# W_q of head 2 read into two places ahead of the gathers, its queries behind head 1's, and head 0's scores copied ahead of half 1's exponentials

## What is computed

```python
def chunk(xc):                      # 128 positions, x2 after its RMS norm
    q = (xc @ w_query).reshape(128, 8, 2, 128)
    sc = jnp.einsum('chpd,hpnd->chpn', q, sub_keys)
    s1, i1 = lax.top_k(sc[:, :, 0], 16)
    s2, i2 = lax.top_k(sc[:, :, 1], 16)
    # the 16 best of the 256 sums s1 + s2 name 16 of 16384 experts
    best, pos = lax.top_k(cand, 16)
    experts = jnp.take_along_axis(cand_idx, pos, axis=-1)
    g = jax.nn.softmax(best, axis=-1)
    h = gelu(einsum('cd,chkd->chk', xc, u[experts]))
    return einsum('chk,chkd->cd', h * g, v[experts])
```

## Time and profile before

| | us |
|---|---|
| median of 3 runs | 840.93 |
| lowest and highest run | 838.71, 841.11 |
| the profiled execution's own time | 836.34 |
| its span, first to last instruction | 834.5 |
| PE busy, of the span | 679.0 (81%) |
| DVE busy | 525.5 (63%) |
| POOL busy | 502.4 (60%) |
| ACT busy | 236.6 (28%) |
| bytes moved by DMA | 297.91 MB, 268.47 of them by the gathers |

### The profile page before, as it was taken

The page is one execution under the profiler, slowest core; times in us unless marked ns, Lnnn a source line. Parts: engine busy times, 40 slices in busy tenths (PEclk is TensorE's granted clock), DMA queues, the critical chain, the costliest instruction groups (busy, mean ns, idle before and its releaser), DMA issues.

```text
span 834.5 us, 7478 instructions
## 1 busy us (share of the span) xinstructions
PE 679.0 (81%) x2205; PEld 369.6 (44%) x2205; DVE 525.5 (63%) x1389; ACT 236.6 (28%) x606; POOL 502.4 (60%) x533
## 2 busy tenths in 40 slices
PE   5999997469978988878888989887776667777776
PEld 4877575435435444335444445443332223333332
DVE  5565169279652867576667676657666757665454
ACT  7567244232311432311212222331212121212110
POOL 5000007447773777777777767777777776777751
PEclk9999998599997999999999999999999999999999
DMA  8955108949999999999999999999999999999994
GB/s 326 310 166 185 53 1 305 376 143 404 409 403 390 400 409 409 407 409 410 408 409 409 409 409 409 411 409 409 409 410 408 410 409 409 409 409 409 409 409 180
DMA packets 92121, 297.91 MB, mean 357 GB/s; under 512 B 8737, under 2 KB 17074, under 8 KB 92082
## 3 DMA queue, kind: packets, MB, share of 16 engines
q0 software_dynamic: 73728, 268.47, 81.5%
q1 hardware_dynamic: 18354, 28.98, 10.1%
HBM read 296.36 MB, written 1.05 MB: 356 GB/s over the span
## 4 chain that ended last, share of the span: by engine, by line
DMA 34%; PE 34%; POOL 15%; issue 7%; DVE 6%; ACT 4%; DVEq 0%; SPq 0%; POOLq 0%; ACTq 0%
DMA v_row<-in_peer_v_dram,expert 23%; PE bank L1372 16%; POOL u_row L446 9%; DMA u_row<-in_peer_u_dram,expert 7%; POOL v_row L457 6%; PE xg L1119 5%; PE bank L1290 4%; DMA wq<-in_peer_w_query_dram 3%; PE bank L1244 3%; DVE u_row L1023 2%; PE bank L1185 1%; PE bank L1168 1%; ACT soft L549 1%; DMA x_sb<-in_x_dram 1%; ACT L700 0%
## 5 line engine op out<-in xcount | busy, mean ns | idle before, releaser
L1372 PE MATMUL bank<-v_row,diag 128*128 128x512 f32 x1000 | 475.7, 622 | 110.8 <-DMA v_row<-in_peer_v_dram,expert 94.7
L1023 DVE CUSTOM_DVE_ANT_0 u_row<-u_row,xg 128x1024 f32<-128x1024 f32 x244 | 296.4, 1220 | 186.2 <-DMA u_row<-in_peer_u_dram,expert 178.5
L1372 PEld LDWEIGHTS bank<-v_row,diag 128*128 128x128 f32 x1000 | 189.3, 198 | 353.9 <-issue 320.1
L446 POOL DMA_INDIRECT u_row<-in_peer_u_dram,expert x256 | 246.4, 962 | 148.0 <-DVE expert L999 70.5
L457 POOL DMA_INDIRECT v_row<-in_peer_v_dram,expert x256 | 241.2, 942 | 113.3 <-issue 56.6
L1290 PE MATMUL bank<-featT,wq 128*128 128x128 f32 x512 | 68.8, 294 | 23.1 <-DMA wq<-in_peer_w_query_dram 22.2
L1290 PEld LDWEIGHTS bank<-featT,wq 128*128 128x128 f32 x512 | 68.3, 210 | 38.0 <-DMA wq<-in_peer_w_query_dram 23.2
L700 ACT ACTIVATE h_gelu<-h_dot 128x4 f32<-128x4 f32 x64 | 12.8, 202 | 251.8 <-DVE h_dot L1023 251.7
L707 ACT ACTIVATE diag<-ident,act_w 128x128 f32<-128x128 f32 x250 | 82.5, 389 | 3.6 <-DVE act_w L1036 3.6
L660 ACT ACTIVATE qT<-bank 128x128 f32<-128x128 f32 x32 | 8.9, 277 | 176.7 <-PE bank L1290 176.7
L356 POOL TENSOR_TENSOR normed<-qk_raw,t_qk_rs 128x512 f32<-128x512 f32 x4 | 4.1, 1047 | 56.6 <-DVE t_qk_rs L896 56.6
(11 more groups left out here) (160 smaller groups left out, 518.0 us busy)
## 6 DMA issues: line engine op xcount, KB each, us to landing
w_raw<-in_w_in_dram SPq DMA_DIRECT2D x12, 1024.0 KB, 7.9
wq<-in_peer_w_query_dram SPq DMA_DIRECT2D x8, 1024.0 KB, 18.1
w_raw<-in_w_out_dram SPq DMA_DIRECT2D x4, 1024.0 KB, 5.1
u_row<-in_peer_u_dram,expert POOLq DMA_INDIRECT x256, 16.5
v_row<-in_peer_v_dram,expert POOLq DMA_INDIRECT x256, 16.6
x_sb<-in_x_dram SPq DMA_DIRECT2D x2, 512.0 KB, 3.8
g_row<-in_norm_g_dram SPq DMA_DIRECT2D x1, 512.0 KB, 12.9
out_dram<-y_rows SPq DMA_DIRECT2D x1, 512.0 KB, 6.7
```

The lines of the kernel that those rows point to most:

```text
L446: pool.indirect_dma_start(u_rows[n % U_RING][:, :], None, peer_u[0], bass.IndirectOffsetOnAxis(ap=expert[:, u, s:s + 1], axis=0))\
L1023: dve.tensor_tensor_reduce(out=row[:, :], in0=row[:, :], in1=x_of, scale=1.0, scalar=0.0, op0=ALU.mult, op1=ALU.add, accum_out=h_dot[:, u ...
L1372: ins = mm(ps[y_bank(h, c)][:, :], diag[:, m % DIAG_RING, :], v_rows[n % V_RING][:, c * COLS:(c + 1) * COLS], start=False, stop=True, skip ...
```

## The change

SP reads W_q of head 2 a second time: into `wq_2`, two parts of 4 KB per partition at the places of x (half 0) and of qt (half 0), as soon as the last transposes of half 0's attention output are done (`mixT_done` 2). PE does `head_queries(2)` directly behind `head_queries(1)` from these parts, and ACT copies its queries and scores directly behind those of head 1. The place of `wq[2]` for half 1 moves to the output projection's weights; those of heads 3 and 4 take the two places that are free after `values_done`. The v row buffers are taken in another order, with other waits on POOL. On ACT `scores_evac(0)` and `scores_evac(1)` go ahead of `exponentials(4)`.

```diff
--- before.py
+++ after.py
@@ -65,6 +65,7 @@
 UNIT_GROUPS = TOPK // GROUP
 SBUF_X_GROUPS = 3
 PROBS = 9
+BATCHES = 12
 PROBS_BANK = [2, 2, 3, 5, 5, 0, 1, 0, 1]
 MIXES_READY = {0: 1, 3: 2, 4: 3}
 MIX_AFTER = {0: 0, 4: 1, 6: 4}
@@ -190,13 +191,14 @@
     diag = Region(sq_at).put("diag", [P, DIAG_RING, P])
 
 
-    wq_at = [wh_at, wl_at, v_at, e_at] + [wr_at + 8 * K * i for i in range(4)]
+    wq_at = [wh_at, wl_at, wr_at, v_at, e_at] + [wr_at + 8 * K * i for i in range(1, 4)]
     wq = [Region(at).put(f"wq{i}", [P, KD, 2 * P]) for i, at in enumerate(wq_at)]
+    wq_2 = [Region(at).put(f"wq2_{c}", [P, KD, P]) for c, at in enumerate((x_at, qt_at))]
 
 
     u_at = [w + 8 * K + 4 * K * i for w in (wh_at, wl_at) for i in range(4)] + [xn_at + 8 * K, xn_at + 12 * K]
     u_rows = [Region(at).put(f"u_row{i}", [P, D]) for i, at in enumerate(u_at)]
-    v_row_at = [skn_at, skn_at + 4 * K, x_at, qt_at, qt_at + 4 * K, kt_at, kt_at + 4 * K, probs_at, scaled_at]
+    v_row_at = [skn_at, skn_at + 4 * K, kt_at, kt_at + 4 * K, qt_at + 4 * K, probs_at, x_at, qt_at, scaled_at]
     v_rows = [Region(at).put(f"v_row{i}", [P, D]) for i, at in enumerate(v_row_at)]
     y_rows = [Region(x_at + 4 * K).put("y_rows0", [P, D]), Region(u_at[0]).put("y_rows1", [P, D])]
     added = Region(u_at[1]).put("added", [P, D])
@@ -217,6 +219,7 @@
         sk_loaded = sem("sk_loaded")
         w_loaded = [sem(f"w_loaded{i}") for i in range(W_LOADS)]
         wq_loaded = [sem(f"wq_loaded{i}") for i in range(PEER_HEADS)]
+        wq_2_loaded = sem("wq_2_loaded")
         g2_loaded = sem("g2_loaded")
         u_landed = [sem(f"u_landed{i}") for i in range(U_RING)]
         v_landed = [sem(f"v_landed{i}") for i in range(V_RING)]
@@ -396,11 +399,15 @@
             sp.wait_ge(w_used, 10)
             query_weights(0)
             query_weights(1)
+            sp.wait_ge(mixT_done, 2)
+            for c in range(2):
+                sp.dma_start(wq_2[c][:, :, :], w_query[0, :, 512 + c * P:512 + (c + 1) * P].rearrange("(k p) n -> p k n", p=P))\
+                  .then_inc(wq_2_loaded, 16)
             sp.wait_ge(values_done, PROBS)
-            query_weights(2)
             query_weights(3)
+            query_weights(4)
             sp.wait_ge(x2_done, 4)
-            for i in range(4, PEER_HEADS):
+            for i in (5, 6, 7, 2):
                 query_weights(i)
 
 
@@ -470,8 +477,12 @@
                     for n in range(g * GROUP - LAG, (g + 1) * GROUP - LAG):
                         if n == 0:
                             pool.wait_ge(skT_done, 4)
-                        if n == 4:
+                        if n == 2:
+                            pool.wait_ge(logits_done, BATCHES)
+                        if n == 5:
                             pool.wait_ge(values_done, PROBS)
+                        if n == 6:
+                            pool.wait_ge(query_done, 6)
                         if n == 8:
                             pool.wait_ge(xg_in_psum, 2)
                             pool.wait_ge(u_used, SBUF_X_GROUPS * GROUP)
@@ -667,9 +678,9 @@
             skT_evac(1)
             query_evac(0)
             query_evac(1)
-            exponentials(4)
             scores_evac(0)
             scores_evac(1)
+            exponentials(4)
             exponentials(5)
             act.wait_ge(late_v_done, 1)
             act.activation(v_sb[:, 0, 1, :], ps[5][:, :], ACT.Copy).then_inc(copied, 1)
@@ -677,6 +688,10 @@
             query_evac(3)
             scores_evac(2)
             scores_evac(3)
+            query_evac(4)
+            query_evac(5)
+            scores_evac(4)
+            scores_evac(5)
             probs_evac(3)
             skT_evac(2)
             exponentials(6)
@@ -718,10 +733,6 @@
                 act.activation(xg[:, c, :], scaled[:, 0, c * COLS:(c + 1) * COLS], ACT.Copy).then_inc(xg_in_psum, 1)
             d_squares(1)
             d_deviation(1)
-            query_evac(4)
-            query_evac(5)
-            scores_evac(4)
-            scores_evac(5)
             for g in range(GROUPS + 1):
                 if g < GROUPS:
                     gelu(g)
@@ -1280,14 +1291,18 @@
 
                 h, hp = query_event(e)
                 i, c = divmod(hp, 2)
-                if c == 0:
+                first = h == 0 and i == 2
+                if first:
+                    pe.wait_ge(wq_2_loaded, 32)
+                else:
                     pe.wait_ge(wq_loaded[i], 16)
                 if e >= 2:
                     pe.wait_ge(scores_ready, e - 1)
                 for k in range(KD):
                     if e == 0 and k % 4 == 0:
                         pe.wait_ge(featT_ready[k // 4], 1)
-                    ins = mm(ps[2 + e % 2][:, 0:P], wq[i][:, k, c * P:(c + 1) * P], featT[h][:, k, :],
+                    part = wq_2[c][:, k, :] if first else wq[i][:, k, c * P:(c + 1) * P]
+                    ins = mm(ps[2 + e % 2][:, 0:P], part, featT[h][:, k, :],
                              start=k == 0, stop=k == KD - 1)
                 ins.then_inc(query_done, 1)
 
@@ -1313,6 +1328,7 @@
             pe.wait_ge(nmax_ready, 6)
             logits(7)
             head_queries(1)
+            head_queries(2)
             pe.wait_ge(copied, 12)
             mixed_transposes(3)
             pe.wait_ge(skT_ready, 2)
@@ -1344,7 +1360,6 @@
             soft_transposes(8, 11)
             values(7, 10)
             values(8, 11)
-            head_queries(2)
 
             def out_step(step):
 
```

## The result

| | before | changed |
|---|---|---|
| median us (lowest to highest, runs) | 840.33 (838.71 to 841.11, 4) | 825.08 (824.64 to 826.01, 4) |
| ratio, 95% interval | | 0.9822 (0.9804 to 0.9841) |
| profiled execution, span | 836.34, 834.5 | 826.01, 824.2 |

The change makes the kernel 15.25 us faster. 826.7 was forecast, with a range of 822.8 to 831.5.

What follows compares the result with a forecast made beforehand. DMA paces the gathers; what can be won is time it isn't full after 125 us. Gain 14.2 us (13.7 from DMA, 15.0 from POOL's issue): 840.93 - 14.2 = 826.7, range 822.8 to 831.5.

Steps and rivals of the forecast that it cites:

- What bounds it: From 188 us on DMA paces the gathers at 390 to 410 GB/s; only earlier time without full DMA can be won.
- The cause of the 18 us: POOL's 18.07 us wait for unit 1's experts comes from head 2's late W_q read, whose ACT copies stand before gelu(0).
- The second read's time and the bytes: Head 2's W_q, read at about 95 us, lands in 18 of 30 us; its added 1 MB costs nothing.
- Scores first: Head 0's scores before the exponentials on ACT: first gather at 123.4 instead of 125.32, 1.9 us eaten by DMA's idle time.
- Queries in the middle: Head 2's queries on PE take 4.7 us, putting the rest of half 1's attention 3.7 us later.
- Sum at DMA: DMA restarts at 178.6 before; after, it works from 141.8 to 164.9: 13.7 us gained, 15.0 by POOL's issue, 14.2 taken.
- The later stall at no cost: PE's 16.80 us wait for head 4's weights at 237.66 and POOL's 7.73 go, for 0 gain (bounds 0 and 1.7).
- A: Late attention costs more: PE's clock falls earlier, delaying chain and DMA's restart 3.7 us; gain about 10.5, 830; chance 0.18.
- B: POOL's 15.0 holds and the 1.7 us at 240 to 284 were PE's stall; gain 16 to 17, 824; chance 0.12.
- C: No change: PE's pace, not DMA's, sets the gathers from 192 to 240, so starting earlier only fills v ring; chance 0.03.
- D: Slower: PE's clock stays low in its full stretch from 182.7 to 237.66; net 26 slower, about 853; chance 0.03.
- my signs of being wrong: Hole near 140 over 6 us, DMA stop beside it, POOL v-buffer wait 200 to 230, or DMA under 405 GB/s.

Runs made afterwards that it cites:

- e6: The kernel before with only head 2's four ACT copies moved behind the diagonals of columns 0 to 3: 828.10 us, ratio 0.9855.
- e10: The changed kernel with head 2's queries and their copies back at their old places, the early read kept: 821.99 us, ratio 0.9786.
- e12: The changed kernel with exponentials(4) ahead of head 0's scores again, as before: 824.19 us, ratio 0.9811.
- e8: The changed kernel with six useless matmuls in PE's waits between 133 and 142 us to hold the clock: 824.64 us, ratio 0.9814.
- e9: The kernel before, unchanged, timed and profiled again: 839.32 us, ratio 0.999.
- e11: The changed kernel with head 4's W_q read in the late batch behind x2: 824.67 us, ratio 0.9815.
- e5: The changed kernel once more, unedited: 824.91 us, ratio 0.9812 to the kernel before at 841.01.
- e1: Same kernel as e10, on the slower chip: 900.66 us against 912.17 for the kernel before, ratio 0.9865.
- e7: The kernel before with head 2's W_q read at 120 us, its queries behind column 3, head 0's scores first, head 4's read early: 820.31 us, ratio 0.9767.

## Why the prediction was right, by its own steps

*What bounds it.* Right, as the table of lost DMA time shows: ten executions of eight kernels have 810.0 to 811.7 us beside it.

*The cause of the 18 us.* Right, and shown by e6: the four ACT copies in front of gelu(0). e10 shows that the other end of the same wait, the late read, is as good a place to cut it.

*The second read's time and the bytes.* Right: 4.8 us to land against 30 to spare. The Trainium skill (DMA: Bandwidth & Descriptors, Specifications) puts the least transfer for line rate at 512 B, and the trace agrees: two parts of half a megabyte in runs of 512 B took a median of 4.8 us from issue to landing, where two of 1 MB in runs of 1 KB took 8.9.

*Scores first.* 1.8 us at the first gather (125.32 to 123.50) and 0 in time; e12 agrees.

*Queries in the middle.* 4.7 us were forecast on PE; 125.43 to 129.92 is 4.5. The attention was forecast 3.7 us late. It was about so for dots(0), which free the eleventh gather's buffer (139.70 seen, 140.1 forecast), but the last logits began 5.3 us late (144.06 against 138.80). The granted clock was 0.50 already from 136 to 140, where before it was 0.92; with the clock held in e8 the same logits began at 141.34. The 25th gather came at 163.52 for 161.95. What these queries cost in time is shown by e10: 2 to 3 us.

*Sum at DMA.* This is the term that was mis-sized. The hole near 140 cost nothing against before, whose eleventh gather I had placed 2.3 us too early: to 144 us 6.0 us were lost before and 5.9 after. I let DMA run full from 141.8 on. But in the changed kernel the stretch from 144 to 168 had 333 GB/s and lost 4.5 us (2.3 before), nearly all of it ahead of 160. My sum let DMA work on 2 MB of W_q from 141.8 on, but SP's timeline has these reads issued at 155.73, when the last value product was done (before, the late read was issued at 150.47). Until then DMA had only what POOL gave it, with three long issues and a wait: from 144 to 160 POOL began eleven gathers, enough for 360 GB/s, and DMA moved 302 at a share of 0.88. Why it wasn't 360 isn't shown. The 24th gather, forecast at 156.8, went out at 159.65. The gain from the profiled execution was thus 10.3 us and not 14.2 (11.1 by the lost time, 23.6 less 12.5). That the medians gave 15.25 is owed to the other side, half of it shown: the profiled execution of before had lost less than e9's (26.0). Two errors, of 3.9 and 4.9 us and of opposite sign, stand behind a forecast that is 1.6 us off, so that it lies this near is luck.

*The later stall at no cost.* Right, e11. But only PE's wait went. POOL still waited for v buffers behind 240, 3.96 us at the most (ahead of the gather at 277.10), with DMA at a share of 1.04.

*The rivals.* A: the clock fell earlier, as it says, at a price too small to measure (e8). B: fallen (e11). C and D: PE was full from 192 to 240 at a clock of 1.00, DMA too, and POOL waited 1.03 us for a v buffer there, once, ending at 224.39. Such a wait between 200 and 230 was among my signs of being wrong; DMA kept its share of 1.03 through it. D's price was wrong by its own numbers: 40 us lost less the 14.2 gained is 26 above the kernel before, 867 us, and not 853, which takes the gain off twice. The granted clock was 0.50 up to 160, 0.60 from 160 to 164 and 1.00 behind it; PE had begun the first columns at 158.28. The Trainium skill (TensorE: Matmul & The Clock Gate, Part 1) says activity lifts the throttle, and the trace agrees.

## What to carry to other kernels

When a part is paced by DMA, count the time in which DMA isn't full, stretch by stretch, and judge every edit by that sum; here it gave the span of every kernel to 1.7 us, and showed a 17 us stall of PE to be worth 0.3 us of DMA time. Look for instructions that wait for late data and stand in front of others on their queue that don't need it: four copies put behind one group of work gave 12.9 us, most of the 16.1 that the whole change gave on the same chip. And forecast from more than one execution of the kernel before: the one that was profiled lay 4 us under its median.

## What the runs showed of the hardware

- One chip took 912.17 us for the kernel before, the others 841.01 and 840.54. From 284 us on DMA moved 409 GB/s at a share of 1.03 in the changed kernel and in e5 to e12. On the slower chip it wasn't a lower rate of a full DMA. This is e1, in two stretches:

```profile
284.00:350.00 66.00, 53.78 (x160) 27.80 (x160) 41.64 (x116) 13.48 (x42) 42.59 (x46) 0.85 1.02 404
350.00:450.00 100.00, 78.64 (x242) 41.00 (x243) 54.18 (x158) 20.53 (x63) 61.62 (x67) 0.88 0.94 348
```

  At a share of 1.02 it moved 404 GB/s there too, and 348 where the share was 0.94 (the average from 284 to 700 is 360). The four executions on that chip have waits with the releaser "remote" in this part, up to 24.8 us for one of ACT's copies of queries in e1; the ten on the others have none. What holds the engines up isn't shown. A ratio is worth more than a time.
- POOL's indirect DMAs take 0.94 us to issue, and some 1.97 to 1.99 us. In the changed kernel the long ones between 124 and 192 us (three of 1.68 to 1.99 up to 152, one behind) fall on DVE's first twelve dot products, whose x is in SBUF (e7: 135.47 above); with x in PSUM every gather from 192 to 284 takes 0.93 to 0.97. That the two go together is seen; the reason was not tried.
- An activation table load took 1.28 us and the next instruction followed 0.01 to 0.02 us later in each place read here.
